# First unit's transposes and gate product laid between the shared down products, a shorter routing chain, and the end placed inside the last step

## The chip, the cores and the metric

One core of a Trainium2 chip runs one program. The metric is device time in microseconds (us) of one execution. A span is the time from the first to the last instruction in a profiled execution.

## The reference

One layer of a trunk over 384 tokens (128 context, 256 latent), model width 1024, in fp32. Ahead of the change's place stand an adaptive norm, an input projection, three mixers (attention, short convolution, recurrent scan), their gates and an output product. The change is about the last part:

```python
h = h + gate1 * mix
n2 = RMSNorm(h) * (1 + scale2) + shift2
s = sigmoid(n2 @ w_router); sel = s + b_router      # 64 experts in 8 groups of 8
# group score = sum of its two best; the 4 best groups stay; of their experts the 8 best
# weight = s / sum(s of the 8) * 2.5
y  = sum over the 8 experts: (silu(n2 @ w_gate[e]) * (n2 @ w_up[e]) * weight) @ w_down[e]
sh = (silu(n2 @ w_sh_gate) * (n2 @ w_sh_up)) @ w_sh_down
h  = h + gate2 * (y + sh)
out = RMSNorm(h) * final_g
```

Each expert has 256 hidden columns and 3 MB of weights.

## The kernel before

**Programs.** Each engine has a program written by hand, all with explicit semaphores. Up to the expert loop they follow one list, `SCHEDULE` (lines 167 to 225): each entry is a stage, and each engine runs its share of each stage in the list's order. `link` makes an instruction wait for the one before it on its engine.

**Tokens and tiles.** The 384 tokens are three tiles of 128 (`NT` = 3). A product of fp32 is two TensorE instructions of the profile, one of fp32r (rounded) is one.

**Routing.** `norm_t` m transposes the normed tile and VectorE modulates it into nT (line 1482). `route` makes the router products, `router` the sigmoid (ScalarE, line 960) and the choice of groups and experts (VectorE, 1490 to 1531), `counts` the number of tokens of each expert, from which VectorE (1534 to 1563) makes a table of units. `table_t` and `table` turn it into positions on TensorE; the same entry makes the numbers of the experts and the count of units, which VectorE writes into ROW (1567 to 1569). ROW is read into registers by all engines (`unit_count`) and by SyncE for each weight load (lines 661 to 669). `rows` m writes the tile's modulated rows to memory (line 957), from where tokens are gathered. `index` u (TensorE 1700, VectorE 1147 and 1148) computes unit u's token indices from one-hot rows that VectorE makes ahead (`one_hots`, 1137 and 1138).

**Shared expert.** `sh_up` m is its gate and up product in 8 pieces, used as filling work between routing stages; `sh_silu`, `sh_hid` follow. `sh_down` m is: transposes of the hidden rows (TensorE, 2019), copy HT (ScalarE, 979), product (TensorE, 2025), copy SHO[m] (ScalarE, 981). GpSimd then multiplies SHO[m] with the gate rows (1085) and adds it to the residual XH (1086), and counts `sh_added`.

**Units.** A unit is one block of up to 128 tokens of one expert, or two half blocks of 64 tokens of two experts. Units come in the order large, large, pair; there are 40 here. Their weights lie in four slots: 0 and 1 for the large ones, 2 and 3 for a pair. Slot 2 holds the shared weights first, so its first load waits for the last shared product (`shd_ready`). Gate and up weights of the unit three ahead are loaded when a unit's gate product is done, down weights when its down product is done.

**The loop.** Step i (from 1) on TensorE: transposes of the gathered tokens of unit i+1 (2031), first half of the gate product of unit i (2045, or 2047 and 2048 for a pair), transposes of the hidden rows of unit i-1 (2086), index products of unit i+4 (1700), second half of the gate product, down product of unit i-1 (2060 to 2062 for a large unit, in three rounded products of high and low parts; 2070 and 2071 for a pair). ScalarE: high part of the down weights of unit i-1 into DNH (1002), copy XT of the transposed tokens (985), copy of the hidden rows (1012), SiLU (989). DNH lies in bigC where SHO[0] and SHO[1] were, so the first high part waits for `sh_added` 2 (line 999). VectorE: one-hots for the index of unit i+4, low part of the down weights (1604), indices, low part of the hidden rows (1609), hidden product (1594), weighting of the down product into YS (1628). GpSimd: gather of unit i+3 (1068), scatter of YS (1098).

**GpSimd before its loop** (lines 1072 to 1088): gathers 0 and 1; a memset; gather 2; after the first transposes gather 3, which needs the indices of unit 3; then the three pairs of multiply and add for SHO. These lines are not in the diff.

**The end** (lines 1638 to 1682 and 2113 to 2139). The scattered parts are loaded back as twelve YG pieces, four for each token tile (703). The last two units' rows are not scattered: one-hots OHT (1672) place them by a TensorE product (`kept_rows`). Part of the pieces is summed on TensorE (`loaded_rows`, 2119), part on VectorE (1644, 1647). `residual` (1653 to 1655) and `final_norm` (1662 to 1666) follow for each tile, and a store (706). All this stands behind the loop.

## Time and profile before

| what | us |
|---|---|
| median of 3 runs | 1113.5 |
| lowest and highest run | 1106.01, 1113.51 |
| profiled execution, its own time | 1105.11 |
| its span | 1103.3 |
| TensorE busy in the span | 1046.7 (95%) |
| VectorE, ScalarE, GpSimd busy | 531.1, 355.2, 166.0 |

The loop begins near 594 and ends near 1061. A busy TensorE is not TensorE at its peak, since matmuls are pipelined and their ends are modelled. Line numbers are those of the kernel before. A row of the timeline gives start, duration, engine, line, operation, what it writes and reads, shapes and count; in brackets the idle time before it and what ended it.

### The profile page before, as it was taken

What the parts mean: (1) busy time and instruction counts of PE and PEld (TensorE: products, weight loads), DVE (VectorE), ACT (ScalarE), POOL (GpSimd) and SP (SyncE); (2) the same over time, 40 slices, a digit from 0 to 9 for tenths busy, and PEclk for the clock granted to TensorE, in tenths of its full rate; (3) what the DMA queues carried; (4) which work ended last, traced back from release to release, by engine and by line L of the source; (5) the groups of instructions that cost most, each with busy time, mean ns of one, the idle gap of its engine ahead of it and who ended that gap; (6) DMA issues with size and microseconds to landing.
All of it is one profiled execution on the core that took longest, in us unless ns stands there. A gap on an engine that the chain in (4) does not pass through costs nothing.

```text
span 1103.3 us, 15100 instructions
## 1 busy us (share of the span) xinstructions
PE 1046.7 (95%) x4876; PEld 702.0 (64%) x4876; DVE 531.1 (48%) x1110; ACT 355.2 (32%) x476; POOL 166.0 (15%) x142
## 2 busy tenths in 40 slices
PE   4999999999899999999998999999999999999975
PEld 2489888788788897874645455555555555454532
DVE  2233544355698956944633434433344334333358
ACT  3333544326444445501322222222222222222101
POOL 0020232000000000000015222322322212111100
PEclk9999999999999999999999999999999999999998
DMA  9999777346555332740249999999999999999692
GB/s 354 395 293 356 114 117 106 136 175 213 202 185 184 116 117 96 240 160 0 97 195 409 383 405 399 416 412 398 415 415 417 410 404 418 416 408 383 243 405 109
DMA packets 88529, 306.62 MB, mean 278 GB/s; under 512 B 13398, under 2 KB 17750, under 8 KB 66464
## 3 DMA queue, kind: packets, MB, share of 16 engines
q1 hardware_dynamic: 68896, 270.63, 62.2%
q0 software_dynamic: 12256, 26.80, 10.5%
q10 hardware_dynamic: 7328, 8.55, 2.2%
q8 instruction: 29, 0.48, 0.2%
q14 instruction: 20, 0.16, 0.0%
HBM read 285.31 MB, written 36.85 MB: 292 GB/s over the span
## 4 chain that ended last, share of the span: by engine, by line
PE 60%; DVE 2%; issue 1%; ACT 1%; DVEq 0%
PE PS L2045 17%; PE PS L2047 8%; PE PS L2070 4%; PE PS L1944 4%; PE PS L2031 3%; PE PS L1691 3%; PE PS L2060 3%; PE PS L2062 2%; PE PS L2061 2%; PE PS L2002 1%; PE PS L2119 1%; PE PS L2086 1%; PE PS L1932 1%; PE PS L1933 1%; PE PS L1934 1%
## 5 line engine op out<-in xcount | busy, mean ns | idle before, releaser
L1098 POOL DMA_INDIRECT y_parts<-bigB,IDX x38 | 72.3, 1902 | 323.8 <-DVE bigB L1628 314.7
L2045 PE MATMUL PS<-bigB 128*128 128x512 f32 x224 | 102.3, 600 | 0.0
L1745 PE MATMUL PS<-bigB_r 128*128 128x384 f32 x288 | 98.6, 342 | 1.3 <-ACT bigB L790 1.3
L2047 PE MATMUL PS<-bigA,bigB 128*64 128x512 f32 x208 | 94.7, 598 | 3.3 <-issue 3.3
L1747 PE MATMUL PS<-bigB_r,bigA_r 128*128 128x384 f32 x288 | 96.5, 335 | 0.0
L1746 PE MATMUL PS<-nT_r,bigB_r 128*128 128x384 f32 x288 | 96.3, 334 | 0.0
L2048 PE MATMUL PS<-bigB 128*64 128x512 f32 x208 | 94.8, 598 | 0.0
L2045 PE MATMUL PS<-bigA,bigB 128*128 128x512 f32 x208 | 94.6, 597 | 0.0
L1628 DVE TENSOR_SCALAR bigB<-PS,bigD 128x1024 f32<-128x1024 f32 x40 | 51.3, 1284 | 89.2 <-PE PS L2062 55.0
L1237 DVE TENSOR_TENSOR bigA_r<-bigA,bigB_r 128x2048 fp32r<-128x2048 f32 x18 | 41.3, 2292 | 97.5 <-ACT bigB_r L816 97.5
L1594 DVE TENSOR_TENSOR bigB<-bigB,PS 128x256 f32<-128x256 f32 x40 | 16.9, 422 | 134.3 <-ACT bigB L989 134.3
L790 ACT ACTIVATE bigB<-PS 128x384 f32<-128x384 f32 (+1 forms) x55 | 27.3, 497 | 145.9 <-PE PS L1747 70.1
L2045 PEld LDWEIGHTS PS<-bigB 128*128 128x128 f32 x224 | 40.9, 192 | 41.0 <-issue 40.9
L1759 PE MATMUL PS<-bigC_r,bigA_r 128*128 128x384 f32 x192 | 65.5, 341 | 0.0
L2045 PEld LDWEIGHTS PS<-bigA,bigB 128*128 128x128 f32 x208 | 37.5, 191 | 37.3 <-issue 37.3
L985 ACT ACTIVATE bigB<-PS 128x1024 f32<-128x1024 f32 x40 | 40.7, 1017 | 62.6 <-PE PS L2031 62.6
L989 ACT ACTIVATE bigB<-PS 128x256 f32<-128x256 f32 x40 | 15.4, 384 | 140.0 <-PE PS L2045 98.0
L1745 PEld LDWEIGHTS PS<-bigB_r 128*128 128x128 f32 x288 | 54.0, 188 | 7.4 <-issue 4.3
L2047 PEld LDWEIGHTS PS<-bigA,bigB 128*64 128x64 f32 x208 | 26.3, 136 | 49.2 <-issue 47.8
L1746 PEld LDWEIGHTS PS<-nT_r,bigB_r 128*128 128x128 f32 x288 | 54.1, 188 | 0.0
L1747 PEld LDWEIGHTS PS<-bigB_r,bigA_r 128*128 128x128 f32 x288 | 54.0, 188 | 0.0
L2060 PE MATMUL PS<-bigC_r,bigB_r 128*128 128x512 f32 x108 | 49.8, 461 | 3.6 <-DVE bigB_r L1609 3.6
(372 smaller groups left out, 2127.2 us busy)
## 6 DMA issues: line engine op xcount, KB each, us to landing
bigA<-in_w_in SPq DMA_DIRECT2D x17, 2048.0 KB, 11.0
bigB<-in_w_gate SPq DMA_DIRECT2D x27, 1024.0 KB, 11.0
bigB<-in_w_up SPq DMA_DIRECT2D x27, 1024.0 KB, 18.9
bigB<-in_w_down SPq DMA_DIRECT2D x27, 1024.0 KB, 19.0
bigA<-in_w_gate SPq DMA_DIRECT2D x26, 1024.0 KB, 8.2
bigA<-in_w_up SPq DMA_DIRECT2D x26, 1024.0 KB, 16.6
bigA<-in_w_down SPq DMA_DIRECT2D x26, 1024.0 KB, 19.2
bigA<-in_w_ada SPq DMA_DIRECT2D x8, 2048.0 KB, 10.0
```

Of the source, the lines that this page charges most:

```text
L1098: pool.indirect_dma_start(y_parts, bass.IndirectOffsetOnAxis(ap=IDX[:, p, 1:2], axis=0), YS[:, p % 2, :], None, bounds_check=T * TOPK - 1, ...
L1628: nc.vector.tensor_scalar(YS[:, p % 2, :].rearrange("p (a n) -> p a n", a=2), PS[:, 6:8, :], WC[:, p:p + 1], None, ALU.mult).then_inc(ys_d ...
L1745: mm(out, wh, nh, start=(k == 0), stop=False)
L1746: mm(out, wh, nl, start=False, stop=False)
L1747: last = mm(out, wl, nh, start=False, stop=(k == KD - 1))
L1759: last = mm(out, low[:, k, :], NHI2[:, k, :], start=False, stop=(k == KD - 1))
L1944: last = mm(PS[:, 6 + hf, :], G[:, k, m * P:(m + 1) * P], w[:, k, :], start=(k == 0), stop=(k == KD - 1))
L2045: last = mm(PS[:, 2 + b, :], XT[:, b, k, :], GU_W[s][:, :, k, :], start=first, stop=stop)
L2047: mm(PS[0:HALF, 2 + b, :], XT[:, b, k, 0:HALF], GU_W[2][:, :, k, :], start=first, stop=stop)
L2048: last = mm(PS[HALF:P, 2 + b, :], XT[:, b, k, HALF:P], GU_W[3][:, :, k, :], start=first, stop=stop)
L2060: mm(out, HTH[:, b, k, :], DNH[:, k, cols], start=(k == 0), stop=False)
L2070: mm(PS[0:HALF, 6 + hf, :], HT[:, b, k, 0:HALF], DN_W[2][:, k, cols], start=(k == 0), stop=(k == 1))
```

## The change

The order of the routing part and the shared expert:

```diff
           ("late_high", "br", 3), ("late_high", "src", 2)] + [("late_high", "br", i) for i in range(4, 7)]
     s += [("late_act", 2), ("gates_out",), ("late_high", "br", 7), ("branches",), ("mod2",), ("wout", 0, 0), ("wout", 0, 1), ("norm2", 0), ("wout", 1, 0),
           ("wout", 1, 1), ("norm2", 1), ("norm_t", 0), ("wout", 2, 0), ("norm_t", 1), ("wout", 2, 1),
-          ("norm2", 2), ("rows", 0), ("route", 0), ("route", 1), ("norm_t", 2), ("rows", 1), ("sh_up", 0, 0, 2),
-          ("route", 2), ("router",), ("rows", 2), ("sh_up", 0, 2, 8), ("sh_silu", 0), ("sh_up", 1, 0, 3), ("counts",),
-          ("sh_up", 1, 3, 8), ("sh_silu", 1), ("sh_hid", 0), ("sh_hid", 1), ("sh_up", 2, 0, 3), ("table_t",),
-          ("sh_up", 2, 3, 5), ("table",), ("sh_up", 2, 5, 8), ("sh_silu", 2), ("index", 0), ("sh_down", 0), ("sh_hid", 2),
-          ("index", 1), ("sh_down", 1), ("index", 2), ("sh_down", 2), ("index", 3)]
+          ("norm2", 2), ("route", 0), ("route", 1), ("sh_up", 0, 0, 1), ("norm_t", 2), ("route", 2), ("router",),
+          ("rows", 0), ("sh_up", 0, 1, 4), ("rows", 1), ("sh_up", 0, 4, 7), ("counts",), ("rows", 2),
+          ("sh_up", 0, 7, 8), ("sh_silu", 0), ("sh_up", 1, 0, 4), ("row",), ("table_t",), ("sh_up", 1, 4, 5), ("sh_hid", 0),
+          ("table",), ("sh_up", 1, 5, 8), ("sh_silu", 1), ("index", 0), ("sh_hid", 1), ("index", 1), ("sh_up", 2, 0, 8),
+          ("sh_silu", 2), ("sh_down", 0), ("index", 2), ("sh_hid", 2), ("first_t",), ("sh_down", 1), ("first_gu",), ("sh_down", 2),
+          ("index", 3)]
     return s
 
 
```

`first_t` is the first unit's transposes, `first_gu` its whole gate product; `row` the two small products for ROW, taken out of `table`. Buffers: DNH becomes two, `[cut(bigC_r, 0, (2, D)), cut(bigD_r, 0, (2, D))]`; OHT and ACC and the last YG piece move. Shared down products use banks 5, 6 and 7 where they used 3, 1 and 2. Of tile 2, VectorE modulates the first four column blocks and ScalarE the other four (activation Identity with scale and bias), each counted alone, and `route` 2 takes them one by one; ScalarE runs a Sigmoid on one spare element behind the root of `norm2` 2. SyncE waits for `n2_out` and `row_done` and reads the count of units only after the loads into slots 0, 1 and 3.

VectorE's choice of groups: the comparisons of all pairs of groups (six operations of 64 columns and four further ones) are replaced by

```diff
+                        ins = nc.vector.max(GB8[:, m, :], GS[:, m, :])
                     link(ins)
...
+                    link(nc.vector.memset(GB8[:, :, TOPG:8], 3e38))
+                    for m in range(NT):
+                        ins = nc.vector.match_replace(GK[:, m, :], GB8[:, m, :], GS[:, m, :], -3e38)
+                    link(ins)
+                    link(nc.vector.tensor_tensor(GK, GK, GS, ALU.not_equal))
```

and the mask is applied by one minimum instead of multiply and add; the weights and ranks are computed after the mask is handed on. In `counts` 22 links become 12, and the count is read from PSUM directly.

ScalarE around the loop:

```diff
             units = unit_count(act)
-            take_xt(0, 0)
             take_xt(1, 1)
-            silu(0, 0)
-
-            def down_high(turn, i, s):
+
+            def down_high(turn, s):
                 act.wait_ge(dn_loaded[s], 16 * turn)
-                if s == 0:
-                    act.wait_ge(sh_added, NT - 1)
-                else:
-                    act.wait_ge(dn_ready, i - 1)
-                nc.scalar.activation(DNH, DN_W[s], ACT.Copy).then_inc(dn_high, 1)
+                nc.scalar.activation(DNH[s], DN_W[s], ACT.Copy).then_inc(dn_high, 1)
+
+            act.wait_ge(sh_added, NT - 1)
+            down_high(1, 0)
 
             def step(i, p):
 
                 act.wait_ge(gu_ready, i)
-                if p % 3 < 2:
-                    down_high(pas * 4 + (p // 3 + 1), i, p % 3)
                 with act.If(i + 2 <= units):
                     take_xt(i + 1, p % 2)
                 act.wait_ge(ht_ready, i)
                 nc.scalar.activation((HTH if p % 3 < 2 else HT)[:, p % 2, :, :], PS[:, 5, 0:2 * P].rearrange("p (k t) -> p k t", k=2),
                                      ACT.Copy).then_inc(ht_done, 1)
                 with act.If(i + 1 <= units):
+                    if (p + 1) % 3 < 2:
+                        down_high(pas * 4 + ((p + 1) // 3 + 1), (p + 1) % 3)
                     act.wait_ge(hid_done, i)
                     silu(i, (1 + p) % 2)
 
```

VectorE before the loop and in a step (the old step is in the listing above):

```diff
             take_index(AHEAD, AHEAD, AHEAD % 3)
+            dve.wait_ge(sht_ready, NT)
             hidden(0, 0)
             units = unit_count(dve)
 
-            def down_low(p):
-                if p % 3 < 2:
-                    dve.wait_ge(dn_high, pas * (BODY // 3 * 2) + (p // 3 * 2 + p % 3 + 1))
-                    nc.vector.tensor_tensor(DNL[p % 3], DN_W[p % 3], DNH.bitcast(F32), ALU.subtract).then_inc(dn_low, 1)
+            def down_low(nth, s):
+                dve.wait_ge(dn_high, nth)
+                nc.vector.tensor_tensor(DNL[s], DN_W[s], DNH[s].bitcast(F32), ALU.subtract).then_inc(dn_low, 1)
+
+            down_low(1, 0)
 
             def hidden_low(i, p):
...
+            def step(i, p):
+
+                u = 1 + p + AHEAD
+                with dve.If(i + 1 <= units):
+                    one_hots(pas * 8 + u // 3 * 2, u % 3, u % 2)
+                    take_index(i + AHEAD, u % BODY, u % 3)
+                    hidden_low(i, p)
+                    if (p + 1) % 3 < 2:
+                        down_low(pas * (BODY // 3 * 2) + ((p + 1) // 3 * 2 + (p + 1) % 3 + 1), (p + 1) % 3)
+                    dve.wait_ge(ht_ready, i)
+                    hidden(i, (1 + p) % 2)
+                    nc.vector.tensor_copy(TOKF[:, p % 2:p % 2 + 1], IDX[:, p, 0:1])
+                    weigh(i, p)
+                with dve.Else():
+                    chain[0] = in_loop
+                    hidden_low(i, p)
+                    link(nc.vector.tensor_copy(TOKF[:, p % 2:p % 2 + 1], IDX[:, p, 0:1]))
+                    dve.wait_ge(ys_done, i)
+                    for b in range(2):
+                        for m in range(NT):
+                            ins = nc.vector.tensor_scalar(OHT[:, b, m, :], kc(K_R128), TOKF[:, b:b + 1], float(-P * m),
+                                                          ALU.subtract, ALU.is_equal)
+                    ins.then_inc(oht_done, 1)
+                    dve.wait_ge(xg_t, i)
+                    two_rows(0, 0)
+                    one_row(0, 1, 0)
+                    weigh(i, p)
+                    last_sums()
```

VectorE's `last_sums` follows there, with the row sums dealt differently: for tile 0 pieces 0, 1 and 2 on VectorE and piece 3 on TensorE; tile 1 pieces 2 and 3 on VectorE; tile 2 pieces 0 and 1 on VectorE, gated and added to XH ahead of `final_norm(1)`, and TensorE's part behind it. On TensorE:

```diff
 
-            pe.wait_ge(sho_done, NT)
-            transposes(1, 0)
             pe.wait_ge(xt_done, 1)
             transposes(1, 1)
             index(AHEAD, AHEAD % 3, AHEAD % 2)
-            gate_up(0, 1, 0, range(KD))
+            pe.wait_ge(sho_done, NT)
             units = unit_count(pe)
 
             def hidden_t(i, p):
...
+
+            def last_sums(i):
+
+                pe.wait_ge(oht_done, 1)
+                pe.wait_ge(ys_done, i + 1)
+                kept_rows(0, True, False)
+                loaded_rows(0, 3, False, True).then_inc(part_ready, 1)
+                kept_rows(1, True, False)
+                loaded_rows(1, 0, False, False)
+                loaded_rows(1, 1, False, True).then_inc(part_ready, 1)
+                kept_rows(2, True, False)
+                loaded_rows(2, 2, False, False)
+                loaded_rows(2, 3, False, True).then_inc(part_ready, 1)
+
+            def finish_unit(i, p):
+
+                pe.wait_ge(ht_done, i)
+                pe.wait_ge(ys_done, i)
+                down(pas * 4 + (p // 3 + 1), p)
 
             def step(i, p):
 
...
                     gate_up(i, turn, 1 + p, range(4, KD))
+                    finish_unit(i, p)
                 with pe.Else():
                     hidden_t(i, p)
-                pe.wait_ge(ht_done, i)
-                pe.wait_ge(ys_done, i)
-                down(pas * 4 + (p // 3 + 1), p)
+                    finish_unit(i, p)
+                    last_sums(i)
 
             with pe.Fori(0, PASSES) as pas:
                 with pe.If(pas * BODY + 1 <= units):
```

`down` reads `DNH[s]` instead of `DNH`. The old `loaded_rows(0, 0)`, `kept_rows` and so on behind the loop are gone. GpSimd's program is unchanged.

## Rows read from the trace of the kernel before

**Rows 1.** The page, 40 slices: busy tenths of DMA.

```profile
DMA  9999777346555332740249999999999999999692
```

**Rows 2.** Chain of waits, 604 to 642: start us, us, engine, line.

```profile
606.36 0.89 PE PS L2031 x8
...
641.25 0.78 PE PS L2031 x7
```

**Rows 3.** Table by stage: PE, PEld, DVE, ACT, POOL busy, clock, DMA share, GB/s.

```profile
921.00:956.00 35.00, 35.00 (x146) 18.28 (x144) 13.35 (x30) 8.87 (x11) 7.00 (x6) 1.00 1.01 416
```

**Rows 4.** Landings: line 665 in 594:600, line 669 in 600:700, in 900:1000.

```profile
DMA to landing us min/median/max: 14.1/14.1/14.1
...
DMA to landing us min/median/max: 10.7/14.4/17.0
...
DMA to landing us min/median/max: 22.7/25.2/27.2
```

**Rows 5.** Timeline, 940 to 1050, ScalarE's high parts, and a TensorE step's opening.

```profile
996.76 1.91 ACT L1002 ACTIVATE bigC_r<-bigA 128x2048 fp32r<-128x2048 f32 x1 [7.73 <-DMA bigA<-in_w_down]
...
1031.86 1.91 ACT L1002 ACTIVATE bigC_r<-bigA 128x2048 fp32r<-128x2048 f32 x1 [5.75 <-DMA bigA<-in_w_down]
...
1028.25 1.05 PE L2031 MATMUL PS<-K,bigB 128*128 128x128 f32 x8
```

**Rows 6.** Waits, 940 to 1010, TensorE: total us, times, longest.

```profile
PE PS L2047 <- issue: 3.3, 2, 2.1
```

**Rows 7.** Timeline of TensorE, 580 to 607: start us, us, then idle before.

```profile
581.76 1.16 PE L2031 MATMUL PS<-K,bigB 128*128 128x128 f32 x8 [0.89 <-ACT nT L981]
...
586.30 7.65 PE L2045 MATMUL PS<-bigB 128*128 128x512 f32 x16
...
599.57 0.49 PE L1700 MATMUL PS<-bigD_r,bigC_r 128*128 128x8 f32 x3 [1.08 <-DVE bigD_r L1138]
...
606.20 1.05 PE L2031 MATMUL PS<-K,bigB 128*128 128x128 f32 x8
```

**Rows 8.** Timeline of GpSimd, ScalarE and VectorE, 583 to 600.

```profile
583.80 0.99 POOL L1068 DMA_INDIRECT bigB<-n_rows,IDX  x1 [5.67 <-PE PS L2031]
...
584.80 2.37 POOL L1085 TENSOR_TENSOR bigC<-bigC 128x1024 f32<-128x1024 f32 x1
...
591.98 2.35 POOL L1086 TENSOR_TENSOR bigB<-bigB,bigC 128x1024 f32<-128x1024 f32 x1
...
594.46 1.91 ACT L1002 ACTIVATE bigC_r<-bigB 128x2048 fp32r<-128x2048 f32 x1
...
596.79 2.31 DVE L1138 CAST bigD_r<-bigD_r 128x9 fp32r x1
```

**Rows 9.** Timeline of the routing part, 539 to 566.

```profile
539.52 0.33 ACT L960 ACTIVATE bigD<-PS 128x192 f32<-128x192 f32 x1 [0.66 <-PE PS L1691]
...
549.88 7.08 PE L2002 MATMUL PS<-bigA,nT 128*128 128x512 f32 x16
...
564.88 0.36 SPq L664 DMA_DIRECT2D bigB<-in_w_gate  x1
```

**Rows 10.** Timeline of the end, 1046 to 1103.

```profile
1055.20 0.79 PE L2060 MATMUL PS<-bigC_r,bigB_r 128*128 128x512 f32 x1 [3.59 <-DVE bigB_r L1609]
...
1052.54 2.28 DVE L1604 TENSOR_TENSOR bigB_r<-bigB,bigC_r 128x2048 fp32r<-128x2048 f32 x1
...
1059.84 1.28 DVE L1628 TENSOR_SCALAR bigB<-PS,bigD 128x1024 f32<-128x1024 f32 x1 [4.63 <-PE PS L2062]
...
1065.34 1.26 DVE L1672 TENSOR_SCALAR bigC<-K,small 128x128 f32<-128x128 f32 x6 [4.21 <-issue]
...
1067.77 5.00 DVE L1647 TENSOR_TENSOR bigC<-bigC,bigA 128x1024 f32<-128x1024 f32 x4
...
1083.13 17.47 SPq L706 DMA_DIRECT2D out_y<-bigB  x3
```

**Rows 11.** Table by stage, TensorE alone: busy, granted clock, DMA share, GB/s.

```profile
1056.00:1058.00 2.00, 2.00 (x6) 0.50 1.01 426
```

More of the change, by code:

```diff
@@ L353, in trunk @@
         HTL = cut(bigB_r, 12288, (2, 2, P))
-        DNH = cut(bigC_r, 0, (2, D))
+        DNH = [cut(bigC_r, 0, (2, D)), cut(bigD_r, 0, (2, D))]
         DNL = [cut(bigB_r, 4096, (2, D)), cut(bigA_r, 10240, (2, D))]
@@ L678, in _ @@
                 down_of(r, q)
+            units = unit_count(sp)
             sp.wait_ge(shd_ready, NT)
@@ L948, in _ @@
                     nc.scalar.activation(small[:, 8 + m:9 + m], small[:, 4 + m:5 + m], ACT.Sqrt).then_inc(root2, 1)
+                    if m == NT - 1:
+                        nc.scalar.activation(small[:, 84:85], small[:, 83:84], ACT.Sigmoid)
+                elif st == "norm_t" and ev[1] == NT - 1:
+                    m = ev[1]
+                    act.wait_ge(mod_ready, 3)
+                    act.wait_ge(n2_ready, m)
+                    act.wait_ge(xnt2, 2 * m + 2)
+                    for k in range(4, KD):
+                        nc.scalar.activation(nT[:, k, m * P:(m + 1) * P], PS[:, 1, k % 4 * P:(k % 4 + 1) * P], ACT.Identity,
+                                             bias=modc[:, 2, 1, k:k + 1], scale=modc[:, 3, 1, k:k + 1]).then_inc(xt_copied, 1)
                 elif st == "rows":
@@ L1564, in _ @@
                     dve.wait_ge(tab_ready, 1)
-                elif st == "table":
+                elif st == "row":
                     dve.wait_ge(pr_ready, 1)
@@ L1631, in _ @@
-            with dve.Fori(0, PASSES) as pas:
-                with dve.If(pas * BODY + 1 <= units):
-                    for p in range(BODY):
-                        i = pas * BODY + (1 + p)
-                        with dve.If(i <= units):
-                            step(i, p)
-            def rows_of(m, chunks):
-                for n, c in enumerate(chunks):
-                    i = 4 * m + c
-                    dve.wait_ge(y_back[i], 32 if i < EARLY else 16)
-                    if n == 0:
-                        link(nc.vector.tensor_tensor(ACC, YG[i][:, 0, :], YG[i][:, 1, :], ALU.add))
-                    else:
-                        for r in range(2):
-                            link(nc.vector.tensor_tensor(ACC, ACC, YG[i][:, r, :], ALU.add))
+            two = lambda a: a.rearrange("p (a n) -> p a n", a=2)
@@ L1685, in _ @@
+            with dve.Fori(0, PASSES) as pas:
+                with dve.If(pas * BODY + 1 <= units):
+                    for p in range(BODY):
+                        i = pas * BODY + (1 + p)
+                        with dve.If(i <= units):
+                            step(i, p)
         @block.tensor
@@ L1701, in index, with transposes, gate_up @@
                 last.then_inc(ix_ready, 1)
+            def transposes(turn, b):
+                pe.wait_ge(gathered[b], 16 * turn)
+                for k in range(KD):
+                    last = nc.tensor.transpose(PS[:, k // 4, k % 4 * P:(k % 4 + 1) * P], XG[b][:, k:D:KD], ident)
+                last.then_inc(xg_t, 1)
+            def gate_up(u, turn, p, ks):
+                b, s = p % 2, p % 3
+                if 0 in ks:
+                    pe.wait_ge(gu_loaded[s], 32 * turn)
+                    if s == 2:
+                        pe.wait_ge(gu_loaded[3], 32 * turn)
+                    pe.wait_ge(xt_done, u + 1)
+                for k in ks:
+                    first, stop = k == 0, k == KD - 1
+                    if s < 2:
+                        last = mm(PS[:, 2 + b, :], XT[:, b, k, :], GU_W[s][:, :, k, :], start=first, stop=stop)
+                    else:
+                        mm(PS[0:HALF, 2 + b, :], XT[:, b, k, 0:HALF], GU_W[2][:, :, k, :], start=first, stop=stop)
+                        last = mm(PS[HALF:P, 2 + b, :], XT[:, b, k, HALF:P], GU_W[3][:, :, k, :], start=first, stop=stop)
+                if KD - 1 in ks:
+                    last.then_inc(gu_ready, 1)
             for ev in SCHEDULE:
@@ L1966, in _ @@
                     pe.wait_ge(wo_taken, 2 * NT - 1)
-                    pe.wait_ge(n2_ready, m + 1)
-                    product(PS[:, 6, m * NE:(m + 1) * NE], lambda k: nT[:, k, m * P:(m + 1) * P], lambda k: WR[:, k, :], KD).then_inc(rt_ready, 1)
+                    if m < NT - 1:
+                        pe.wait_ge(n2_ready, m + 1)
+                    for k in range(KD):
+                        if m == NT - 1:
+                            if k < 4:
+                                pe.wait_ge(n2_ready, NT + k)
+                            else:
+                                pe.wait_ge(xt_copied, KD + k - 3)
+                        last = mm(PS[:, 6, m * NE:(m + 1) * NE], nT[:, k, m * P:(m + 1) * P], WR[:, k, :], start=(k == 0), stop=(k == KD - 1))
+                    last.then_inc(rt_ready, 1)
                 elif st == "counts":
```

262 lines of the change are left out of this document (120 added, 142 removed).

## The prediction

> **What bounds the kernel now.** I read the page first. The slice line of DMA [rows 1] shows three stretches: a busy start, a middle in which the queues are nearly idle, and from the routed experts on a flat line at 9. The change touches only what lies behind the middle, so I cut there.
>
> The chain of waits is next. In the expert loop it is TensorE all the way, and its repeating piece is exact: the transposes that open a step lie at 606.36 and, three steps on, at 641.25 us [rows 2]. Three steps (two large units and one pair of half units) take 34.9 us, eleven and a half times for 40 units.
>
> But the table by stage says that DMA is as full as TensorE: share 1.01 in 921 to 956 [rows 3]. Which of the two leads is seen in the time from issue to landing of the down weights: median 14.4 us in 600 to 700, 25.2 us in 900 to 1000 [rows 4]. The backlog grows by about 1.3 us per three steps. Late in the loop it shows: ScalarE sits 7.73 and 5.75 us idle until down weights land [rows 5], and TensorE itself loses 3.3 us at two places, both at the first gate product of a half-unit step [rows 6]. So the loop is TensorE's with almost no slack in DMA.
>
> Before the loop TensorE has small holes (0.89 us at the first transposes, and others like it), one hole of 1.08 us in step 1 at the index products, and step 2 opens at 606.20 [rows 7]. The end is VectorE's: from 1065.34 to the last store it works nearly without a hole [rows 10].
>
> **Part 1, the routing chain.** The sigmoid stood at 539.52 [rows 9]. With the last modulation split between VectorE and ScalarE and the table of the sigmoid loaded early I put it at 537.0. The group selection loses about 1.6 us of small operations, the round table about 1.2 us by fewer links, and the round numbers no longer wait for the table products. Set against TensorE's queue, which holds the same shared products in other places, the numbers are on ROW at 552.7 and the first expert weights are issued at 553.6 instead of 564.88 [rows 9], 11.3 us earlier. That is worth nothing by itself: TensorE's holes ahead of the loop and in step 1 are not for weights [rows 7], and the only ones that are come after 940 [rows 6], and the next slot (number 2, which holds the shared weights) still waits for the last shared product. The early weights only fill three slots sooner; DMA then idles from about 577 to 591.
>
> **Part 2, transposes and gate product between the shared down products.** TensorE's work is the same. It only changes order: before, index 3 ended at 580.9, followed by transposes (0.93) and the gate product (16 instructions of 0.43, as in the 7.08 of [rows 9], 6.9 us). These 7.8 us now lie ahead of index 3. The round trips of the shared part are partly filled, but new ones open: the first transposes wait for the third shared hidden (1.1), ScalarE copies in the order SHO, XT, HT (1.4 before the second down product, 0.85 before the third), the table products wait for their operands (0.7) and index 1 for index 0 (0.4). Net 2.3 us more. Index 3 then ends at 580.9 + 7.8 + 2.3 = 591.0; step 1 opens at 593.2 instead of 593.78, and its index products are reached at 597.9 instead of 599.57.
>
> **Part 3, what hangs on index 3.** This is the step on which my forecast rests. GpSimd's program is unchanged: gather 3, which needs index 3, stands ahead of the six products and sums that add the shared output. Before, it ran at 583.80, the sums began at 584.80, and the second was done at 591.98 + 2.35 = 594.33 [rows 8]. Now gather 3 can run only at 591.2, the sums begin at 592.2, and the second ends 9.5 us later, at 601.7. ScalarE's high part of the first down weights (into DNH[0], where SHO lay) waits for it, as before: it started at 594.46 and took 1.91 [rows 8]; now 601.8 to 603.7. The VectorE half (2.28 [rows 10]) used to stand behind the one-hots of step 1; the change puts it ahead of the loop, so **the one-hots for unit 5 are queued behind it**, and TensorE's index products of step 1, with the second half of the gate product behind them, wait for these.
>
> At the earliest the one-hots are there at 603.7 + 2.3 + 0.9 = 607.0. GpSimd's last two operations run until 606.5 meanwhile. The row 596.79 [rows 8] shows what that does: a cast of 9 columns took 2.31 us and ended with GpSimd's sum. The Trainium skill says of this, in SBUF — State Buffer, section SBUF: two separate sides, that VectorE and GpSimd share one port pair as "an exclusive lock, not a bandwidth split". By that rule, and the trace agrees with its 2.31 us, two VectorE operations can each wait out one of GpSimd's. From the row alone: up to 2.8 us more, so 609.8 at the latest; I take 609.3, since the low part reads SBUF twice and is ready just as GpSimd's next operation starts. From the index products to the opening of step 2 it is 606.20 - 599.57 = 6.6 us [rows 7]. TensorE has been idle for some 11 us by then; after an idle 3.59 us its clock was at 0.50, the lower level [rows 10, 11], and seven products took 0.43 instead of 0.23, so 1.7 us here. Step 2 opens at 609.3 + 0.1 + 6.6 + 1.7 = 617.7: **11.5 us later**. Bounds: 8.8 (no port, full clock) and 14.
>
> **Part 4, the loop.** The 1.91 us of ScalarE and 2.28 us of VectorE move from the start of the next step to the middle of this one, in time that both spent waiting; each step issues the same. What changes is when down weights must be there: the high part now stands ahead of the SiLU of the same step. Before, they could land 3.6 us after the step that uses them opened (ScalarE took them at 1031.86 in a step that opened at 1028.25 [rows 5], and TensorE did not stop). Now landing + 1.9 + 2.3 + 0.4 of hidden product must precede the hidden transposes, 4.4 us into the step: landing by 0.5 us before it opens, 4.1 us tighter. Unit 37 landed 3.6 late with 3.3 us of stalls already taken: 6.9. Against it the queue is emptier after the stall of part 3: the up weights issued at 595.1 landed 14.1 us later [rows 4], so DMA still had 4.8 us to do when the next ones were issued at 604.5 (TensorE's second gate product done), and later some 1 us idle; now no backlog, and about 2.9 idle. So lateness shrinks by 2.9, to 4.0, and the stall is 4.0 + 0.5 = 4.5 instead of 3.3: **1.2 us more**. Bounds: 0 and 4.1.
>
> **Part 5, the end.** The low part no longer stands in the last step: VectorE had it between 1052.54 and 1054.8, and TensorE idled 3.59 [rows 10]. The last down product starts at 1053.2 instead of 1055.20 and the weighting ends at 1058.4 instead of 1061.1. The 4.21 us in which VectorE ran out of the loop [rows 10] go, as does the first TensorE sum. Then TensorE has 16 instructions of 0.43 to the first partial sum (1065.5) and 24 to the second (1075.8). VectorE from there: residual 3.7, three row sums 3.7, gate and sum 2.5, norm 2.7, to 1088.5; last two 2.5; square 1.3 and root with its fix 1.6; scaling 1.3: 1095.2, where it was 1100.2. Less some half-clock time, **4.5 us earlier**. Bounds: 2.5 and 6.5. The loads of the parts land every 2.5 us as before, ahead of each use.
>
> **Sum.** 11.5 + 1.2 - 4.5 = +8.2 us, against the profiled execution of 1105.1 (span 1103.3): 1113.3. The median shown is 1113.5, 8.4 above that execution, with runs from 1106.0 on; I carry the difference to the median: 1121.7.
>
> **Rivals.** (a) The wait of part 3 doesn't bind, since GpSimd's sums come early enough or VectorE passes it. Then step 2 opens 1.3 us early, the queue term is +0.9, the end -4.5: -5, 1108.5, not slower. For it: every other effect of the change is a gain. Against: the order gather 3, sums, high part, low part, one-hots is written in the four programs, and the rows have each duration. (b) The new deadline of part 4 bites fully: DMA, not TensorE, sets the loop, and no relief comes from the emptier queue. It decides as soon as down weights land over some 19 us after issue, and late in the loop they take 25.2 [rows 4]. 11.5 + 4.1 - 3 = +12.6: 1126, slower by over 1%. (c) The big last step inside each of the 12 copies costs every step a longer jump. At 0.2 us for 39 steps: +8 more, 1130. Against: the jump back over all 12 copies shows no hole now. (d) The change doesn't do what it says: shared round trips are not filled, index 3 at 593 instead of 591: 2 us on top, 1124.
>
> **Chances.** Forecast (with d) 0.68, (a) 0.14, (b) 0.13, (c) 0.05. One per cent, about what a measurement can tell, is 11 us. Of the forecast's own spread (1115 to 1128) about a fifth lies over it; with (b) and (c) that is 0.30 slower. Only the best end of (a), with a full gain at the end, is faster by over 11 us: 0.06. The rest, 0.64, is within 1%, mostly on the slow side. The range takes (b) and reaches down towards (a), and covers that the runs before already differ by 7.5 us: 1109 to 1130.
>
> **What would show it.** Right: weights issued near 553; sums on GpSimd from about 592; a hole of 9 to 12 us on TensorE before the index products of step 1, released by VectorE's one-hots; step 2 at 615 to 619; three steps still 34.9; ScalarE waiting longer for down weights late in the loop; the last store issued 43 us after the last low part of the hidden rows, instead of 45.5. Wrong: if sums start before 586, or index products of step 1 run at 598, part 3 falls and with it the sign.

## The result, and the profile after

The changed kernel takes 1158.5 us (median of 4 runs, 1156.4 to 1162.2) beside 1110.0 us (4 runs) of the kernel before on the same chip: ratio 1.044, 95% interval 1.039 to 1.050. It is slower by 48 us, where 8 were forecast, and outside the range. The profiled execution has a span of 1155.8 us, 52.5 more than the one before.

I cut the span in three where the steps open. The last of the last normed tile's transposes began 3.0 us earlier in this execution (531.45, not 534.41), so the first stretch is counted from there, and these 3.0 us are called the head start below.

| stretch | before | after | difference |
|---|---|---|---|
| last transpose of the normed tiles to opening of step 2 | 71.8 | 84.6 | +12.8 |
| step 2 to step 38 | 422.1 | 452.7 | +30.6 |
| step 38 to the end of the span | 75.1 | 87.1 | +12.0 |

**First stretch.** The timeline of the changed kernel, SyncE, GpSimd, ScalarE, VectorE and TensorE in turn:

```profile
550.55 0.36 SPq L664 DMA_DIRECT2D bigB<-in_w_gate  x1
...
589.03 0.99 POOL L1082 DMA_INDIRECT bigB<-n_rows,IDX  x1 [17.63 <-PE PS L1750]
590.04 2.37 POOL L1099 TENSOR_TENSOR bigC<-bigC 128x1024 f32<-128x1024 f32 x1
...
597.22 2.34 POOL L1100 TENSOR_TENSOR bigB<-bigB,bigC 128x1024 f32<-128x1024 f32 x1
...
601.94 4.27 POOL L1100 TENSOR_TENSOR bigB<-bigB,nT 128x1024 f32<-128x1024 f32 x1
```

```profile
599.59 1.91 ACT L1013 ACTIVATE bigC_r<-bigB 128x2048 fp32r<-128x2048 f32 x1 [9.57 <-POOL bigB L1100]
...
601.53 2.48 DVE L1617 TENSOR_TENSOR bigB_r<-bigB,bigC_r 128x2048 fp32r<-128x2048 f32 x1 [11.64 <-ACT bigC_r L1013]
603.94 2.49 DVE L1151 TENSOR_TENSOR bigC_r<-K,bigC 128x192 fp32r<-128x192 f32 x1
...
607.03 0.80 PE L1744 MATMUL PS<-bigD_r,bigC_r 128*128 128x8 f32 x3 [9.58 <-DVE bigD_r L1152]
```

This is the forecast's chain, link by link. The weights are early [rows 9]. GpSimd's sums start 5 us later than in [rows 8] (8 without the head start). Then high part, low part and one-hots follow in a row, and TensorE is idle for 9.58 us where 1.08 stood [rows 7].

**Second stretch.** The pitch, from the opening of a step to that of the next, is 11.21, 11.67 and 12.00 us in turn, so three steps take 34.88 us, as in [rows 2], in nearly all of the stretch. The exceptions are these. At the three places where the loop of 12 steps jumps back, TensorE sits idle, and the profile names no releaser (timeline of TensorE):

```profile
749.95 1.97 PE L1750 MATMUL PS<-K,nT 128*128 128x128 f32 x8 [5.15 <-issue]
...
899.65 1.97 PE L1750 MATMUL PS<-K,nT 128*128 128x128 f32 x8 [5.43 <-issue]
...
1056.26 1.97 PE L1750 MATMUL PS<-K,nT 128*128 128x128 f32 x8 [5.22 <-issue]
```

The clock falls behind each (0.50 from 748.40 to 751.80 in the table by stage). The three pairs of steps around the jumps are longer than their pitch by 7.7, 8.2 and 6.5 us: 22.4 together. "Issue" means that the profile's semaphores explain nothing, so the next view is TensorE's sequencer. The source view of the loop's head (L2201) and of the test of each step (L2205), branches alone, durations in ns as min/median/max:

```profile
L2201 PEldq COMPARE_BRANCH  x8: 83/2403/7591, 741.6 to 1153.3; - x8
...
L2205 PEldq COMPARE_BRANCH  x48: 64/67/4182, 590.1 to 1142.6; - x48
```

The same two in the kernel before:

```profile
L2107 PEldq COMPARE_BRANCH  x8: 83/214/223, 731.1 to 1061.3; - x8
...
L2111 PEldq COMPARE_BRANCH  x48: 64/67/209, 587.1 to 1057.9; - x48
```

A branch that took 0.2 us takes 7.3 to 7.6 at the three jumps back. What it waits for is, as the experiments below show, in the table of DMA queues: the engine's instructions, which are loaded like data. q8 is TensorE's queue and q14 VectorE's. The page's totals (packets, MB, share), of the changed kernel and then of the kernel before:

```profile
q8 instruction: 80, 1.31, 0.5%
q14 instruction: 61, 0.50, 0.1%
```

```profile
q8 instruction: 29, 0.48, 0.2%
q14 instruction: 20, 0.16, 0.0%
```

Of q8's 80 packets 36 fall in 721 to 1120 us; before, 1 fell in 721 to 1060. The rest of the stretch, 8.2 us, are steps that wait for down weights (steps 11, 20, 23, 32 and 35, together 11.6 us over their pitch, before 3.4). The longest, timeline of ScalarE, VectorE and TensorE:

```profile
1022.75 1.91 ACT L1013 ACTIVATE bigD_r<-bigA 128x2048 fp32r<-128x2048 f32 x1 [9.02 <-DMA bigA<-in_w_down]
...
1024.69 2.29 DVE L1617 TENSOR_TENSOR bigA_r<-bigA,bigD_r 128x2048 fp32r<-128x2048 f32 x1 [10.19 <-ACT bigD_r L1013]
...
1027.37 0.51 PE L2143 MATMUL PS<-K,bigB 128*128 128x128 f32 x2 [3.04 <-DVE bigB L1607]
1029.24 0.80 PE L1744 MATMUL PS<-bigD_r,bigC_r 128*128 128x4 f32 x3 [1.37 <-DVE bigD_r L1152]
1029.97 1.11 PE L1766 MATMUL PS<-bigA,bigB 128*64 128x512 f32 x1
```

The gaps are 4.4 us, and the products behind them run at the lower clock (granted 0.50 from 1029 to 1031; 1.11 us, not 0.59).

**Third stretch.** The last down product starts after 1.39 us of idle TensorE, not 3.59 [rows 10]. The three stores:

```profile
1118.32 19.50 SPq L707 DMA_DIRECT2D out_y<-bigB  x3
```

The last is issued at 1137.49, 68.8 us after step 38 opens; before, it was 72.0 [rows 5, 10]. It lands at 1140.1, and the span ends at 1155.8. In those 15.7 us no engine computes. TensorE and VectorE had their last unit in the fourth of the twelve copies and now step over the eight copies left. On TensorE these are seven branches of L2205 of 2.9 to 4.2 us and one of L2201 of 4.58, from 1122.3 to 1150.4. VectorE needs 2.1 to 2.5 us for most copies and 3.6 at the loop's head, and is through at 1155.6. Their fetches (DMA queues, 1141 to 1155):

```profile
q8 instruction: 4, 0.07, 2.3%
q14 instruction: 6, 0.05, 1.4%
```

### The profile page after: what moved, and what is told of

Same layout as the page of the kernel before. It is cut to its first block, busy times and chain, and to the rows that moved or that the text cites. A ratio compares the mean times of both kernels' runs of the same rounds, so it can differ in the third digit from the quotient of the medians.

```text
span 1155.8 us, 15083 instructions
## 1 busy us (share of the span) xinstructions
PE 1057.2 (91%) x4876; PEld 706.3 (61%) x4876; DVE 526.5 (46%) x1105; ACT 357.0 (31%) x481; POOL 132.8 (11%) x142
## 3 DMA queue, kind: packets, MB, share of 16 engines
q8 instruction: 80, 1.31, 0.5%
## 4 chain that ended last, share of the span: by engine, by line
PE 43%; DMA 10%; DVE 4%; issue 3%; ACT 2%; SPq 2%; POOL 1%; DVEq 0%; ACTq 0%
PE PS L1764 10%; DMA bigA<-in_w_down 9%; PE PS L1766 7%; PE PS L2012 4%; PE PS L1735 3%; PE PS L1750 2%; PE PS L2129 2%; PE PS L2080 2%; PE PS L2119 1%; PE PS L2121 1%; PE PS L2120 1%; PE PS L2000 1%; PE PS L2001 1%; PE PS L2002 1%; PE PS L1744 1%
## 5 line engine op out<-in xcount | busy, mean ns | idle before, releaser
L1764 PE MATMUL PS<-bigA,bigB 128*128 128x512 f32 x208 | 102.1, 636 | 0.0
L1766 PE MATMUL PS<-bigA,bigB 128*64 128x512 f32 x208 | 97.4, 612 | 0.0
L1767 PE MATMUL PS<-bigB 128*64 128x512 f32 x208 | 97.4, 612 | 0.0
L1112 POOL DMA_INDIRECT y_parts<-bigB,IDX x38 | 38.2, 1005 | 391.5 <-DVE bigB L1687 372.5
L1161 DVE TENSOR_REDUCE bigD<-PS 128x1 f32<-128x2 f32 (+1 forms) x58 | 9.2, 158 | 130.6 <-PE PS L1744 130.4
L1764 PEld LDWEIGHTS PS<-bigA,bigB 128*128 128x128 f32 x208 | 40.8, 207 | 42.0 <-issue 42.0
L1617 DVE TENSOR_TENSOR bigB_r<-bigB,bigC_r 128x2048 fp32r<-128x2048 f32 x14 | 32.3, 2306 | 50.2 <-ACT bigC_r L1013 50.2
L1617 DVE TENSOR_TENSOR bigA_r<-bigA,bigD_r 128x2048 fp32r<-128x2048 f32 x13 | 29.8, 2291 | 51.6 <-ACT bigD_r L1013 51.6
## 6 DMA issues: line engine op xcount, KB each, us to landing
bigB<-in_w_down SPq DMA_DIRECT2D x27, 1024.0 KB, 18.6
```

Source lines behind the costliest of these rows:

```text
L1617: nc.vector.tensor_tensor(DNL[s], DN_W[s], DNH[s].bitcast(F32), ALU.subtract).then_inc(dn_low, 1)
L1764: last = mm(PS[:, 2 + b, :], XT[:, b, k, :], GU_W[s][:, :, k, :], start=first, stop=stop)
L1766: mm(PS[0:HALF, 2 + b, :], XT[:, b, k, 0:HALF], GU_W[2][:, :, k, :], start=first, stop=stop)
L1767: last = mm(PS[HALF:P, 2 + b, :], XT[:, b, k, HALF:P], GU_W[3][:, :, k, :], start=first, stop=stop)
```

## The experiments

Counted in the built programs, the loop is, in instructions (with the weight loads a product in fp32 counts as four, a rounded one as two, a transpose as two; branches and register work once each):

| kernel | TensorE | VectorE |
|---|---|---|
| before | 1,405 | 301 |
| changed | 3,289 | 1,125 |

The expectations below count transposes as four: for their 1,690, 2,030, 2,680, 3,580 and 3,640 read 1,405, 1,741, 1,909, 3,289 and 2,389. In the changed kernel the end accounts for most of the growth; the rest is that the down product and the weighting stand in both branches. The theory to be tested is that each engine keeps a certain amount of code, and that a loop above it is fetched again at each jump back and for each copy stepped over. The first rival is that DMA backlog makes the holes.

**The end behind the loop, on both engines or on one.** The cut, on TensorE (VectorE alike, its `last_sums()` moved):

```diff
                     finish_unit(i, p)
-                    last_sums(i)
...
                         with pe.If(i <= units):
                             step(i, p)
+            last_sums(units)
```

> The changed kernel with the last sums of TensorE and VectorE behind the loop again; the last step still makes the one-hots OHT and the first two row sums ahead of its weighting. Theory (code size): TensorE's loop falls from some 3,580 instructions of the profile to 2,030, VectorE's from 1,125 to 450; the holes of 5.2 to 5.5 us at the three jumps back and the 15.7 us after the last store go, VectorE's way out of the loop (about 4 us, as in the kernel before) comes back ahead of the last sums: 1122 to 1130. Rival A (the holes at the jumps back are DMA backlog or late weights and have nothing to do with the code): they stay and the time stays at 1150 to 1160. The hole of 9 to 10 us before step 1's index products stays under both.

> Only TensorE's last sums behind the loop, VectorE's stay in every step. Theory (code size, TensorE's alone binds at the jumps back): the three holes go, some 20 us; VectorE still walks over the copies after its last operation, so 10 to 16 us lie between the last store's landing and the end: 1134 to 1142. Rival B (VectorE's code is what stops the loop): the holes stay, 1150 to 1160.

> Only VectorE's last sums behind the loop, TensorE's stay in every step. Theory: the three holes stay at 5 us and more, TensorE's walk over the copies still ends the span; VectorE's walk (some 4 us) now lies ahead of its last sums: 1152 to 1162. Rival B: the holes go and the time falls to 1130 to 1142.

Measured: both 1146.3 us (ratio to before 1.032, 1.028 to 1.035), TensorE's alone 1159.7 (1.042), VectorE's alone 1153.1 (1.039). Only the third is as expected; the second even lies in the range of its Rival B. In the other two TensorE's fetches went (q8 back at 31 packets; in the first run L2200's longest branch is 0.23 us), but a hole came back one step later, on another engine. The first of these runs, VectorE at the jump back, TensorE behind it, and VectorE behind the loop:

```profile
755.13 0.36 DVE L1151 TENSOR_TENSOR bigC_r<-K,bigC 128x192 fp32r<-128x192 f32 x1 [6.24 <-issue]
...
756.05 0.80 PE L1744 MATMUL PS<-bigD_r,bigC_r 128*128 128x8 f32 x3 [3.83 <-DVE bigD_r L1152]
...
1107.02 3.74 DVE L1638 TENSOR_TENSOR nT<-nT,bigA 128x1024 f32<-128x1024 f32 x3 [18.61 <-issue]
```

VectorE's loop, still 453 instructions since the OHT and the first row sums stayed in every step, is fetched too (q14: 41 packets, before 20). In the changed kernel its wait lay beside TensorE's (5.79 us idle at 752.31), so when TensorE's went, VectorE's took its place: the steps behind the jumps are 6.8, 5.7 and 6.6 us too long in the second run. My claim that TensorE's alone binds is refuted; so is the rival that only VectorE's does (the third run keeps its hole of 5.06 us on TensorE). Either engine alone is enough.

**The whole end behind the loop; and with it the sums first.** In both, OHT and the first row sums also move behind the loop (VectorE 281 instructions). The other edit, on GpSimd, was also tried alone on the changed kernel:

```diff
-            gather(GAHEAD, GAHEAD)
             pool.wait_ge(gate_out, 48)
             for m in range(NT):
+                if m == NT - 1:
+                    gather(GAHEAD, GAHEAD)
                 pool.wait_ge(sho_done, m + 1)
```

> The changed kernel with GpSimd's first two multiply-and-add pairs ahead of gather 3; nothing else. Theory of part 3: the first two sums end near 582, the high part of the first down weights and its low part no longer wait, step 1's index products run near 598, step 2 opens near 605 instead of 616: 9 to 12 us less, 1147 to 1150, the holes at the jumps back stay. Rival C (the hole before the index products is not from GpSimd's sums, or the loop takes back what is won since DMA bounds it): less than 4 us won.

> The changed kernel with the whole end behind the loop on both engines, the one-hots OHT and first row sums too: VectorE's loop is 281 instructions (301 in the kernel before, 453 in the first experiment), TensorE's 2,030. Theory (each engine has a size of loop of its own beyond which the jump back fetches code; VectorE's lies between 301 and 453, TensorE's between 2,030 and 3,580): against the first experiment's 1146 the three holes of 6.4 to 6.8 us go (20), and VectorE's 18.6 us on the way out become about 4, less 3 us for what stands behind the loop again (11): 1112 to 1119. Rival D (another reason than VectorE's size, such as the order of low part and one-hots across the jump, makes the hole after it): 1130 or more, with holes of 6 us at the second step of each pass.

> The same with GpSimd's first two sums ahead of gather 3. If the two causes are independent it is 9 to 12 us less than the run before it: 1102 to 1108, below the kernel before. If DMA bounds the loop as soon as TensorE's hole is gone, less than 5 us of it stay: 1110 to 1116.

Measured: sums first alone 1145.7 (1.030), 12.8 us less than the changed kernel; whole end behind alone 1129.0 (1.016, 1.010 to 1.021), 29.5 less; both 1118.2 (1.008, 1.006 to 1.010), 40.3 less, so the causes nearly add (42.3). With the sums first, TensorE's hole before the index products is

```profile
603.02 0.49 PE L1745 MATMUL PS<-bigD_r,bigC_r 128*128 128x8 f32 x3 [0.23 <-DVE bigD_r L1153]
```

With the whole end behind, q14 is back at 20 packets and every step at a jump back has its pitch (12.00 and 11.21 us). But both runs with the end behind miss their expectation by 10 us. It was reckoned from the first of these experiments, in which no other step was over its pitch. Here steps 20, 23, 26, 29, 32 and 35 of the run with both edits last 11.5 us over their pitch (with step 17, 8.7 in the run with the late sums), and ScalarE waits for down weights there. That DMA had caught up in the holes of the jumps would explain it, but isn't shown: the changed kernel has the same holes and 11.6 us over its pitch elsewhere.

**Code that is never executed, in the kernel before.** This is the cleanest test, since nothing of the change is in it.

```diff
                 with dve.Else():
                     down_low(p)
                     hidden_low(i, p)
+                    with dve.If(i >= units + 1):
+                        for _ in range(13):
+                            nc.vector.tensor_copy(TOKF[:, p % 2:p % 2 + 1], IDX[:, p, 0:1])
```

and, in another run, 40 transposes in the same place on TensorE. Two more runs hold 5 of these small copies instead of 13, and 20 transposes instead of 40.

> The kernel before with 13 small copies in the Else of every VectorE step behind a condition that is never true: 485 instructions in the loop instead of 301, none of the new ones executed. Theory: three holes of some 6.5 us at the jumps back (20 us) and VectorE's way out of the loop 18 us instead of 4.2: 30 to 36 us more, 1141 to 1148. Rival D: code that is not executed costs nothing but one branch: 1108 to 1114.

> The kernel before with 40 transposes in the Else of every TensorE step behind a condition that is never true: some 3,640 instructions of the profile in the loop instead of 1,690. Theory: three holes of 5 to 7 us at the jumps back and branches of 3 us over each of the eight unused copies, here ahead of TensorE's last sums (some 26 us, of which VectorE's own work covers part): 35 to 48 us more, 1146 to 1159. Rival D: 1108 to 1114.

> The kernel before with 5 unused copies per VectorE step, not 13: 389 instructions in the loop. Where the size is a threshold, this gives either nothing (1107 to 1113, queue of VectorE's instruction packets at 20 to 25) or the whole, 1130 to 1138; where it is gradual, something between.

> The kernel before with 20 unused transposes per TensorE step, not 40: some 2,680 instructions of the profile in the loop (2,030 made no hole, 3,580 did). Threshold below it: 1140 to 1154; threshold above it: 1107 to 1114, with 29 to 34 packets on TensorE's instruction queue.

| loop, instructions | us | ratio | packets of its queue | idle at first jump back | idle behind the loop |
|---|---|---|---|---|---|
| VectorE 389 | 1134.2 | 1.020 | 38 | 5.07 | 14.43 |
| VectorE 485 | 1133.5 | 1.023 | 41 | 4.77 | 18.99 |
| TensorE 1,909 | 1147.4 | 1.033 | 60 | 3.83 | 27.23 |
| TensorE 2,389 | 1153.6 | 1.037 | 68 | 3.45 | 32.23 |

The first hole at a jump back with the larger addition, on VectorE and then on TensorE:

```profile
740.16 0.36 DVE L1137 TENSOR_TENSOR bigC_r<-K,bigC 128x192 fp32r<-128x192 f32 x1 [4.77 <-issue]
```

```profile
742.70 1.15 PE L2031 MATMUL PS<-K,nT 128*128 128x128 f32 x8 [3.45 <-issue]
```

The transfers of data are those of the kernel before, which has none of these holes, so backlog isn't their cause. The smaller additions cost most of the price of the larger ones (23 of 25 us on VectorE, 36 of 45 on TensorE, each beside the kernel before of its own series), so the price begins at a threshold: for VectorE between 301 and 389 instructions, for TensorE between 1,741 and 1,909. Three of the four runs are as expected. VectorE's 485 came out 7.5 us below the expectation; at the first jump its 4.77 us of idle were only 2.4 for TensorE, which had work left. The way out of the loop is the dearer part (TensorE, 40 transposes):

```profile
1110.60 6.41 PE L2122 MATMUL PS<-bigA,K 128*128 128x512 f32 x8 [32.23 <-issue]
```

The Trainium skill has the mechanism (Runtime: NRT & Kernel Launch, Instruction fetch mechanics): an engine holds 512 instructions, TensorE 2048, refilled in blocks, and "Branching breaks sequential prefetch." The fetches at the jumps back agree. Both thresholds here lie below these figures, as they would if part of a block at either end of the loop also takes room; that reason is an inference. The same section of the Trainium skill speaks of a window of two pages of 256 instructions, and for TensorE that doesn't fit: 1,741 instructions went round with 31 packets in the whole run, where the kernel before has 29.

**The old deadline.** On the run with both edits, the high part goes back to the start of the step that uses it and the low part behind that step's one-hots; and the same without the sums first.

```diff
                 act.wait_ge(gu_ready, i)
+                if p % 3 < 2:
+                    down_high(pas * 4 + (p // 3 + 1), p % 3)
...
-                    if (p + 1) % 3 < 2:
-                        down_high(pas * 4 + ((p + 1) // 3 + 1), (p + 1) % 3)
```

> The run with both ends behind the loop and the two sums first (1118), with the high and low parts of the down weights back where the kernel before has them: high part at the start of the step that uses them, low part behind that step's one-hots. Theory (the earlier deadline of the down weights costs more than forecast): that run lost 11.5 us in steps longer than their pitch, at steps 17, 20, 23, 26, 29, 32 and 35, the kernel before 3.4; with the old deadline some 8 come back, and 1 to 2 are given back at the end, where the low part stands in the last step again: 1108 to 1113. Rival E (DMA bounds the loop either way, since the stalls come from the queue and not from the deadline): 1116 to 1119.

> The same placing of high and low parts, but with GpSimd's sums behind gather 3 as in the changed kernel (compare 1129). Theory: the hole of 9 to 10 us before step 1's index products needs both, sums behind gather 3 and the low part ahead of the one-hots; with the one-hots ahead it goes, and only the down product of step 1 waits, 1 to 4 us: with 8 us from the deadlines 1110 to 1118. Rival F (the late sums alone make the hole): 1119 to 1123.

Measured: 1114.3 (1.004, 1.002 to 1.006) and 1120.8 (1.008, 1.005 to 1.011), the first 1 us above its expectation, the second 3 us above its own and in the range of Rival F. In the first run the steps over their pitch shrink from 11.5 to 3.5 us, as the theory has it; but from the opening of step 38 to the end it is 5.0 us longer than in the run with both edits (to the last landing 80.8 and 75.8), so the gain is 4.0. By its trace the second run refutes Rival F all the same, and shows what the hole of the first stretch needs. TensorE reaches the index products without waiting, and only its down product waits:

```profile
611.31 0.80 PE L2117 MATMUL PS<-bigC_r,bigB_r 128*128 128x512 f32 x1 [3.81 <-DVE bigB_r L1621]
```

It waits 3.81 us, not 9.58: late sums alone cost some 4 us of idle TensorE, and the low part ahead of the one-hots makes 9.6 of it. From the opening of step 1 to that of step 2 it is 12.9 us with the sums first, 18.6 here, and 25.0 in the run with the late sums and the low part ahead.

**The end and the order.** First TensorE's loaded piece ahead of the kept rows again; then, on top, `first_t` and `first_gu` behind `index` 3.

```diff
-                pe.wait_ge(oht_done, 1)
-                pe.wait_ge(ys_done, i + 1)
-                kept_rows(0, True, False)
-                loaded_rows(0, 3, False, True).then_inc(part_ready, 1)
+                loaded_rows(0, 3, True, False)
+                pe.wait_ge(oht_done, 1)
+                pe.wait_ge(ys_done, i + 1)
+                kept_rows(0, False, True).then_inc(part_ready, 1)
```

> The run with everything undone but the routing chain, the new order of the shared part and the new division of the row sums (1114), with TensorE's first loaded piece ahead of the kept rows again, as in the kernel before. In the run it is made from, TensorE waited until 1071.27 for VectorE's one-hots and the last store landed 80.8 us after step 38 opened (before: 74.6). Theory (kept rows first only pays inside the last step, where VectorE does not first walk out of the loop): 4 to 7 us come back, 1107 to 1110, same or up to 0.4% faster than before. Rival G (the new division of the row sums is slower by itself): under 2 us come back.

> The same with the first unit's transposes and gate product behind index 3 again, so that of the change's order only the shorter routing chain is left. By the second part of the forecast the new order costs 2.3 us net on TensorE and opens step 1 no earlier; if so this run is 0 to 3 us faster than the run beside it. Rival H (the new order fills holes as it is meant to): 3 us or more slower.

Measured: 1110.7 (1.000, 0.998 to 1.002) and 1109.2 (0.999, 0.997 to 1.001). The first gives 3.6 us back, a little less than expected; from the opening of step 38 to the last landing it is 77.5 us, of 74.6 before. Undoing the new order takes 1.5 us off by the medians, no difference that can be told. Neither beats the kernel before, so the routing chain, 14 us earlier with its weights, shows no gain here. The one gain that shows is 3.2 us at the stores of the changed kernel (68.8 us after the opening of step 38, not 72.0). It needs the end inside the loop: with the end behind it and all else kept, the last store is issued after 73.2.

## Why the prediction failed

| undone, step by step | us | gain |
|---|---|---|
| changed kernel | 1158.5 | |
| the end out of the loop | 1129.0 | 29.5 |
| sums ahead of gather 3 | 1118.2 | 10.8 |
| old deadline | 1114.3 | 4.0 |
| loaded piece first | 1110.7 | 3.6 |

**Part 1 was right, part 2 nearly.** Weights were issued at 550.6, which with the 3.0 us of head start is the 553.6 of the forecast, and they gained nothing that shows. Index 3 ended at 587.9, forecast 588.0 by the same reckoning. But step 1 opened at 590.97 and its index products were reached at 597.45, with the head start 594.0 and 600.4, where 593.2 and 597.9 were forecast: the wait of 1.67 us for the copied tokens and the slower half of the gate product behind it (4.75 us, not 3.60) were not in the sum. The larger hole behind them hid this.

**Part 3 was right**, in place and size: +12.8 us at step 2, forecast 11.5 (8.8 to 14), and the run with the sums first took 12.8 away by the medians. VectorE and GpSimd held each other up as forecast: the one-hot of 0.34 us took 2.49, and GpSimd's last sum 4.27 instead of 2.35.

**Part 4 was mis-sized.** Forecast +1.2, at most 4.1; measured 8.2 in the changed kernel and 8.0 in the pair of runs on it. The wait was modelled right: in the run with both edits the high part began at 1000.35 and the hidden transposes ran at 1004.97, 4.6 us later, the 1.9 + 2.3 + 0.4 of the forecast. The working has a small slip: 1.9 + 2.3 + 0.4 against 4.4 us gives 0.2 us ahead of the opening, not 0.5. The relief by an emptier queue isn't shown. With the hole in step 1 the steps over their pitch sum to 8.7 us and without it to 11.5, which is the forecast's 2.9; but in the two other pairs of runs it is the other way, 11.6 with the hole and 9.8 without in the changed kernel and the run with the sums first, 4.9 and 3.5 with the old deadline. The term that failed is "4.1 us tighter" as the whole price of the deadline. It costs 8.0 us between the pair of runs, of which 3.1 are idle TensorE (6.5 against 3.3 us in steps 2 to 37); the other 4.9 are time in which it works at the lower clock. Step 35 of the run with both edits has 2.0 us of idle TensorE and is 5.6 us too long, with the clock at 0.50 from 1007 to 1013. In part 3 I had charged the stall with the clock behind it, here not.

**Part 5 was half right.** The stores came 3.2 us earlier in their stretch (forecast 4.5, bounds 2.5 to 6.5): the wait before the last down product shrank by 2.2 us, forecast 2.0, and the rest gave 1.0, forecast 2.5. But the step "the 4.21 us in which VectorE ran out of the loop go" failed. They did not go; they moved behind the end, where the engines still step over the unused copies, and with the larger code they grew to 15.7 us after the last store had landed. I had read 4.21 us of walking in [rows 10] and did not ask where the walk would stand afterwards.

**The miss itself is rival (c)**, to which I gave 0.05. The step of the prediction that failed is that the forecast charged nothing for the larger loop body. Rival (c) named the place (the end inside each of 12 copies) and missed the form and the size, 8 us: not 0.2 us a step, but nothing between the jumps, some 7.5 us at each of three jumps back, and 2.1 to 4.2 us for most of the copies stepped over. With the end out of the loop the kernel takes 29.5 us less. The argument that I set against it, "the jump back over all 12 copies shows no hole now", holds for 1,405 and 301 instructions and says nothing of 3,289 and 1,125. Both could be counted from the kernels; I counted durations and never counted code. The trace of the kernel before had the sign: one packet of TensorE's instructions in 340 us of loop means that its body was kept, and so that there was something to lose.

Rival (a) is refuted by the first stretch, (d) by index 3. Of rival (b) the deadline is borne out, at more than its 4.1 us. One reading ahead of the parts was wrong without changing the sum: three steps come about twelve times between steps 2 and 38, not eleven and a half times in the 40 units.

What stays open: the 2.9 us by which the end is still longer in the run with the loaded piece first, and why single executions of the kernel before range over 9 us. Part of that range can be seen. Three of the four runs with dead code, whose steps 1 are those of the kernel before, open step 2 at 610.5 to 610.9 and not at 606.2. GpSimd starts its gathers 1.2 to 1.4 us later in them, its sums hold up two operations for the one-hots (2.4 and 2.3 us) and not one, and TensorE waits 2.6 us for these, not 1.08, and then works partly at the lower clock. The profiled execution of the kernel before, with 1105.1 us faster than all its other runs, has the short form. The 12.8 us of the first stretch are against that form; against the longer one they would be some 8.3, an estimate from these openings. That is also about what is needed to explain why the spans of the two profiles differ by 52.5 us and the medians by 48.5. Why GpSimd starts later in some executions isn't known.

## What to carry to other kernels

Before work is put inside a loop whose body is written out in copies, count what each engine's body becomes, the untaken branches too: below the engine's limit the jump back shows no hole, above it every jump back and nearly every copy stepped over on the way out costs microseconds, on each engine by itself, and a fix on one engine alone may show nothing. When a wait has "issue" as its releaser, look at the instruction packets among the DMA queues and at the longest branch of the loop's head. And ask of each new stall of TensorE whether a half-clock stretch follows: 2.0 us of idle time cost 5.6 us in one step here, and 2.1 us cost only 2.2 in step 35 of the kernel before.

## What the runs showed that I had not expected

- The size limits above: VectorE fits with 301 instructions and not with 389, TensorE with 1,741 and not with 1,909. TensorE's packets are 16.4 KB (1.31 MB in 80), VectorE's 8.2 KB (0.50 MB in 61).
- In straight flow the fetches are hidden: between jumps the changed kernel fetches code all along, and its steps keep 11.21, 11.67 and 12.00 us.
- Code that is never executed made a kernel 2.0 to 3.7% slower.
- The span can end after the work: 15.7 us of branches behind the last store.
